# Loading the overflow experts of a mixture-of-experts stage from SyncE at a register address

## The reference

```python
g_w, g_idx = lax.top_k(pg, 1)                 # one of 4 groups
e_w, e_idx = lax.top_k(pe, EXP_TOPK)          # two of its 8 experts
for g in range(N_GROUPS):
    h = silu(xf @ w_eg[g]) * (xf @ w_eu[g])   # per expert: 1024 x 128, twice
    out = out + (h * gate) @ w_ed[g]          # per expert: 128 x 1024
```

## Time and profile before

| | |
|---|---|
| median of 3 runs | 1450.25 us (1449.45 to 1452.43) |
| profiled execution, own time | 1453.34 us |
| its span | 1451.5 us |
| PE busy | 1316.5 us, 91% of the span |
| DVE, ACT, POOL busy | 37%, 23%, 15% |
| DMA, mean over the span | 142 GB/s, 205.63 MB |
| mixture steps, layer 0 | about 573 to 709 us |
| mixture steps, layer 1 | about 1280 to 1421 us |

### The profile page before, as it was taken

The page is one execution under the profiler, slowest core; times in us unless marked ns, Lnnn a source line. Parts: engine busy times, 40 slices in busy tenths (PEclk is TensorE's granted clock), DMA queues, the critical chain, the costliest instruction groups (busy, mean ns, idle before and its releaser), DMA issues.

```text
span 1451.5 us, 15494 instructions
## 1 busy us (share of the span) xinstructions
PE 1316.5 (91%) x5756; PEld 729.4 (50%) x5756; DVE 534.1 (37%) x1542; ACT 339.4 (23%) x773; POOL 222.4 (15%) x304
## 2 busy tenths in 40 slices
PE   7999998999999998988699999999999999989780
PEld 5654446544444555655484544564444445556550
DVE  1278885110111137221335779731101113552115
ACT  2142467100000100222213326641000010012121
POOL 5011033000000001223241100600000000023313
PEclk9999999999999997999899999999999999979995
DMA  8302102503303305999662120061060061289966
GB/s 239 116 13 59 58 1 71 174 1 89 128 0 135 154 31 178 396 407 376 233 166 64 45 63 17 20 182 44 0 217 0 0 261 44 85 304 411 406 237 240
DMA packets 95485, 205.63 MB, mean 142 GB/s; under 512 B 26465, under 2 KB 35905, under 8 KB 95409
## 3 DMA queue, kind: packets, MB, share of 16 engines
q1 hardware_dynamic: 80800, 178.13, 34.7%
q0 software_dynamic: 14608, 26.49, 5.2%
HBM read 196.29 MB, written 27.78 MB: 154 GB/s over the span
## 4 chain that ended last, share of the span: by engine, by line
PE 79%; DVE 5%; DMA 4%; ACT 4%; issue 4%; PEld 1%; POOL 1%; PEldq 1%; SPq 0%; POOLq 0%; ACTq 0%; DVEq 0%
PE bank L748 34%; PE bank L1030 10%; PE bank L1081 10%; PE bank L1127 7%; PE bank L1138 4%; PE bank L1114 2%; PE bank L781 2%; DMA uv<-xd,mb 2%; DVE mb L1462 2%; PE bank L830 1%; PE bank L1047 1%; PE bank L734 1%; PE bank L834 1%; PE bank L1122 1%; PE bank L934 1%
## 5 line engine op out<-in xcount | busy, mean ns | idle before, releaser
L748 PE MATMUL bank<-ring,xt 128*128 128x512 f32 (+1 forms) x1120 | 434.0, 544 | 7.9 <-DMA ring<-in_w_in 5.1
L748 PEld LDWEIGHTS bank<-ring,xt 128*128 128x128 f32 x1120 | 214.3, 194 | 209.5 <-issue 190.0
L1751 DVE TENSOR_TENSOR scr<-scr,bank 128x512 f32<-128x512 f32 x20 | 13.7, 687 | 368.6 <-PE bank L1030 368.6
L1081 PE MATMUL bank<-ring,xt 128*128 128x512 f32 x320 | 141.3, 595 | 0.0
L542 POOL TENSOR_SCALAR stat<-stat 128x1 f32<-128x1 f32 (+1 forms) x27 | 11.7, 434 | 796.2 <-ACT uv L1214 614.0
L1358 ACT ACTIVATE scr<-bank,stat 128x512 f32<-128x512 f32 x40 | 25.3, 683 | 347.9 <-PE bank L748 347.9
L1081 PEld LDWEIGHTS bank<-ring,xt 128*128 128x128 f32 x320 | 59.4, 191 | 66.9 <-issue 66.9
L1030 PE MATMUL bank<-ring,att 128*128 128x512 f32 x160 | 72.5, 596 | 2.2 <-ACT sgt L1350 1.8
L781 PE MATMUL bank<-ring,xt 128*128 128x512 f32 x160 | 73.7, 593 | 0.0
L1030 PE MATMUL bank<-ring,sgt 128*128 128x512 f32 x160 | 71.9, 592 | 0.0
L748 PE MATMUL bank<-more,xt 128*128 128x512 f32 x160 | 70.3, 592 | 0.0
(11 more groups left out here) (284 smaller groups left out, 1819.9 us busy)
## 6 DMA issues: line engine op xcount, KB each, us to landing
ring<-in_w_in SPq DMA_DIRECT2D x12, 2048.0 KB, 9.3
ring<-in_w_ed SPq DMA_DIRECT2D x32, 512.0 KB, 17.7
ring<-in_w_eg SPq DMA_DIRECT2D x26, 512.0 KB, 10.5
ring<-in_w_eu SPq DMA_DIRECT2D x26, 512.0 KB, 17.2
ring<-in_w_out SPq DMA_DIRECT2D x4, 2048.0 KB, 12.6
more<-in_w_ed SPq DMA_DIRECT2D x14, 512.0 KB, 10.9
qkv<-in_w_eg SPq DMA_DIRECT2D x12, 512.0 KB, 7.4
qkv<-in_w_eu SPq DMA_DIRECT2D x12, 512.0 KB, 10.1
```

The source lines that it names most:

```text
L748: mm = pe.matmul(out, xt[:, k, t * P:(t + 1) * P], rhs[:, k, :], start=(k == 0), stop=(k == KD - 1))
L1081: mm = pe.matmul(banks[5 + n % 3][:, :], xt[:, k, t * P:(t + 1) * P], w[:, k, :], start=(k == 0), stop=(k == KD - 1))
```

## The change

The loads of units 28 and 29 move from POOL to SP. They stand in SP's order of units, between unit 27 and unit 30, and are plain DMAs whose row is a register: SP waits for `experts_known` before the first refill and loads two expert numbers from `over_expert` into registers. POOL's six indirect DMAs go away, and with them DVE's five operations for `over_rows`; the signal `over_rows_ready` stays and now stands behind the second part of the row table, and POOL waits for it before gather 14. TensorE waits for `up_in` and `down_in` in step 14 as in all others. The load now takes place whether or not there is an overflow unit: `over_expert` is the number of experts that start at or before the unit, less one, which is 31 where there is none.

```diff
-LOADED = [e for e in range(2 * NB) if e // 2 != OVER_AT]
+LOADED = list(range(2 * NB))
...
                 expert(9, EXPERTS * L + 9)
+                sp.wait_ge(experts_known, prior("experts_known", L) + 1)
+                over_row = [sp.value_load(over_expert[:, h:h + 1], min_val=0, max_val=EXPERTS - 1) for h in range(ALWAYS)]
+
+                def row_of(v):
+                    if v // 2 == OVER_AT:
+                        return EXPERTS * L + over_row[v % 2]
+                    return EXPERTS * L + 2 * BLOCK_AT[v // 2] + v % 2
+
                 for e in range(PLACES, 2 * NB, 2):
-                    units = [v for v in (e, e + 1) if v in LOADED]
+                    units = [v for v in (e, e + 1) if v < 2 * NB]
                     for v in units:
                         sp.wait_ge(gu_psum[L], (v - PLACES) // 2 + 1)
-                        expert_up(v % PLACES, EXPERTS * L + 2 * BLOCK_AT[v // 2] + v % 2, up_in[v % PLACES])
+                        expert_up(v % PLACES, row_of(v), up_in[v % PLACES])
                     for v in units:
                         sp.wait_ge(y_psum[L], (v - PLACES) // 2 + 1)
-                        expert_down(v % PLACES, EXPERTS * L + 2 * BLOCK_AT[v // 2] + v % 2, down_in[v % PLACES])
-                sp.wait_ge(experts_known, prior("experts_known", L) + 1)
+                        expert_down(v % PLACES, row_of(v), down_in[v % PLACES])
...
                 for b in range(NB):
+                    if b + XBUF == OVER_AT:
+                        pool.wait_ge(over_rows_ready, L + 1)
                     if b + XBUF < NB:
                         pool.wait_ge(h_done[L], b + 1)
                         gather(b + XBUF, b % XBUF, x_in[b % XBUF])
                     pool.wait_ge(y_ready[L], b + 1)
                     scatter(b, b % XBUF, b % YBUF, y_out[b % YBUF])
-                    if b == OVER_AT - PLACES // 2:
-                        pool.wait_ge(over_rows_ready, L + 1)
-                        for v in range(ALWAYS):
-                            i = (2 * OVER_AT + v) % PLACES
-                            for dst, w, landed_sem in ((places[i][0][:, 0:1024], "w_eg", more_up),
-                                                       (places[i][0][:, 1024:2048], "w_eu", more_up),
-                                                       (places[i][1], "w_ed", more_down)):
-                                rows = (a[w].rearrange("l g e f d -> (l g e f) d") if w == "w_ed" else
-                                        a[w].rearrange("l g e (p k) f -> (l g e p) (k f)", k=KD))
-                                pool.indirect_dma_start(out=dst, out_offset=None, in_=rows,
-                                                        in_offset=bass.IndirectOffsetOnAxis(ap=over_rows[:, v:v + 1], axis=0),
-                                                        bounds_check=DEPTH * EXPERTS * P - 1, oob_is_err=False
-                                                        ).then_inc(landed_sem, 16)
...
-                        if b != OVER_AT:
-                            pe.wait_ge(up_in[e % PLACES], 32 * filled(e % PLACES, L, e))
-                        else:
-                            pe.wait_ge(more_up, 32 * ALWAYS * (L + 1))
+                        pe.wait_ge(up_in[e % PLACES], 32 * filled(e % PLACES, L, e))
...
-                few = [P, ALWAYS, EXPERTS]
-                then(V.tensor_tensor(over_hot, over(start[:, 0:EXPERTS], ALWAYS, 1, few),
-                                     ids[:, 0:ALWAYS].unsqueeze(2).broadcast_to(few), ALU.is_le))
-                V.tensor_scalar(over_none, ids[:, 0:ALWAYS], start[:, EXPERTS:EXPERTS + 1], NOWHERE, ALU.is_ge, ALU.mult)
-                then(V.tensor_reduce(over_begun, over_hot, AX.X, ALU.add))
-                then(V.scalar_tensor_tensor(over_begun, over_begun, float(P), over_none, ALU.mult, ALU.add))
-                V.tensor_scalar(over_rows, over_begun, ids[:, BR:BR + 1], float(P * (EXPERTS * L - 1) - 1),
-                                ALU.add, ALU.add).then_inc(over_rows_ready, 1)
+                V.nop().then_inc(over_rows_ready, 1)
```

More of the change, by code:

```diff
@@ L259, in build @@
         n_over = ALWAYS + 2 * REST
[L260 to L263, removed]
         over_expert = mbv(AT_OVER, n_over)[0:1, :].bitcast(I32)
@@ L324, in build @@
         x_over, y_over = sem("x_over"), sem("y_over")
-        more_up, more_down, over_rows_ready = sem("more_up"), sem("more_down"), sem("over_rows_ready")
+        over_rows_ready = sem("over_rows_ready")
         params, ln_loaded, wr_loaded = sem("params"), sem("ln_loaded"), sem("wr_loaded")
@@ L1175, in down_step @@
                         e = 2 * b + h
[L1176 to L1179, removed]
+                        pe.wait_ge(down_in[e % PLACES], 16 * down_loads(e % PLACES) * filled(e % PLACES, L, e))
                     down(two_of(b), b % 2)
```

## The result

| | before | after |
|---|---|---|
| median | 1451.34 us (1448.56 to 1456.65, 6 runs) | 1461.65 us (1460.73 to 1464.79, 6 runs) |
| ratio to before | 1 | 1.0071 (95% interval 1.0054 to 1.0087) |
| profiled execution, span | 1451.5 us | 1463.0 us |

A forecast was written before the change was run, and what follows sets the result against it. Weight traffic through full DMA engines was taken as the bound in the mixture steps. Layer 0: 7.8 - 0.65 - 0.9 + 1.5 = 7.7 us; layer 1: 3.9 - 0.3 = 3.6; together 11.3, from 1450.25 to 1461.5 us, range 1454 to 1467.

The forecast's parts named there:

- The bytes: Overflow loads per layer go from 0 and 1 to 2 and 2, adding 3.15 MB and 1.57 MB; chance 0.84 that this decides.
- The price of the bytes: Added loads ahead of units 30 to 33, at 403 GB/s, delay later weights 7.8 us in layer 0, 3.9 in layer 1.
- The empty packets: Dropping POOL's out-of-bounds gather packets frees DMA time: 0.65 us gained in layer 0, 0.3 in layer 1.
- The slack of 0.9 us: In layer 0 unit 33's last weights land 0.9 us before the last up projection, absorbing that much delay.
- POOL at nothing: Removing POOL's six indirect DMAs ahead of gather 14 gains nothing, since weights bind behind it; up to 3.8 us otherwise.
- SP and DVE at nothing: SP's wait, register loads and extra issues, and DVE's five dropped operations, were costed at nothing.
- TensorE's clock: Layer 0's last step runs at the slow clock after a wait, costing 1.5 us; layer 1 already pays it.
- The sum: Both layers' mixture steps: 7.7 us later in layer 0 and 3.6 in layer 1, together 11.3 us.
- No change: Rival: the added loads are hidden by room in the drain at the steps' end, time 1450 us; chance 0.07.
- POOL as the bound: Rival: POOL's weight gathers hold up gather 14, so removing them saves 3.8 us, time 1446.5 us; chance 0.05.
- SP can't keep up: Rival: register-address loads hold SP so its DMA queue runs dry, some 5 us more, 1466 to 1470 us; chance 0.04.

The follow-up runs named there:

- e3: Kernel before, with POOL's indices always in bounds so POOL loads two overflow experts per layer; 1464.13 us, ratio 1.0091.
- e5: Changed kernel with a constant row (expert 31 of the layer) instead of the register for units 28 and 29; 1462.76 us, ratio 1.0071.
- e1: Changed kernel with the loads of units 28 and 29 left out; 1447.18 us, ratio 0.9971.
- e2: Kernel before, with POOL's six indices always beyond the bound, so no overflow weights move; 1448.41 us, ratio 0.9987.
- e7: Changed kernel with the two dropped semaphores more_up and more_down declared again, unused; 1462.19 us, ratio 1.0068.
- e8: Changed kernel with DVE's five operations per layer for over_rows put back, result unread; 1462.78 us, ratio 1.0073.
- e6: Changed kernel with each load of units 28 and 29 under a branch on SP, issued only if that overflow unit exists; 1451.27 us, ratio 1.0000.
- e10: Kernel before with POOL's six weight gathers one step later, behind gather 14; 1457.52 us, ratio 1.0029.
- e9: Changed kernel with DVE's five operations and six indirect DMAs per layer on POOL put back, moving nothing; 1466.08 us, ratio 1.0098.
- e4: Changed kernel without the loads of unit 29, so one overflow expert per layer; 1452.95 us, ratio 1.0016.

## Why the prediction was right, point by point

**The bytes.** Right. Layer 0's POOL queue moves 9.09 MB before and after, so it held no overflow weights. e3 shows that the loss comes with the bytes from either queue (from POOL's by another path, through gather 14), e5 that it doesn't come with the register, e1 that it goes with the bytes.

**The price of the bytes.** Forecast 7.8 - 0.65 us later landing in layer 0 and 3.9 - 0.3 in layer 1; in the profiles it is 8.6 and 4.2, or 4.2 to 4.3 us per added expert where I took 3.9. The Trainium skill's figure (DMA: Bandwidth & Descriptors, Specifications), with which I had estimated 8.8 and 4.4, came nearer to these two landings, although the engines move 405 GB/s from 656 to 690 us in the changed kernel too. It isn't a general rate: the same bytes by POOL (e2 to e3) come 7.1 and 6.1 us later for two, 3.3 us per expert, and by the ratios 15 us for four experts, 3.8 each. By SP (e1 to after) the landings of the two layers move by 17.3 us together for four experts, 4.3 each, while the ratios give only 14.5 us, 3.6 each; PE's lateness in e1 hides 3.7 us. So at the landing an expert costs 4.2 to 4.3 us in SP's queue and 3.3 in POOL's, around the 3.9 of 403 GB/s, and why the two differ was not found out. That the time of the kernel is near 3.9 per expert isn't a confirmation of the rate.

**The empty packets.** I had credited 0.65 and 0.3 us for them. 864 packets without data went away in layer 0 (5184 to 4320). From before to after no gain can be seen: the landings are later than 3.9 us per expert would make them. The one pair with equal bytes points the forecast way: without the empty packets (e1) unit 33 lands 0.2 and 1.2 us earlier than with them (e2). But kernels of equal work differ by as much (120.3 to 121.9 in after, e5, e7 and e8). Not shown.

**The slack of 0.9 us.** Right: the last up projection starts at the landing in both layers.

**POOL at nothing.** Right in the mixture: e6, which frees POOL at the bytes of before, gains nothing there, nor does e1 against e2 (1.7 us slower), and in layer 0 of e10 the wait moves from the gather to the weights. It holds only while POOL's gathers carry few weights; with two experts in them, in e3, gather 14 is on the chain. And the step overlooked that fewer DMAs on POOL shorten the end of the program, by 2.9 us (e9 against e8). That is one of the two largest errors of the sum (the other is the clock, below), and both favour the change.

**SP and DVE at nothing.** Right (e5, e8).

**TensorE's clock.** This step failed in its size and place. I gave layer 0 the 1.5 us that the slow clock cost in layer 1 before. In the changed kernel the last step has a granted clock of 1.00, the 2.4 GHz level, in layer 0, and in both layers takes 6.85 us from up to down, so layer 0 lost nothing and layer 1 gained 1.45 us. The waits ahead of it are 1.34 and 1.53 us, where it was 2.79 in layer 1 before. In the other runs it took 6.85 us after waits of 0.3 to 2.7 us, and in e8, after 2.9 and 3.2 us, 8.4 and 9.8 us, with a granted clock of 0.50, the 1.2 GHz level, for the first 2.4 and 5.5 us (below, layer 1). So in these traces the penalty comes and goes with how long PE waits there, which I could not have taken from one row.

```profile
1416.50:1422.00 5.50, 5.50 (x39) 5.50 (x41) 0.00 (x0) 0.00 (x0) 0.00 (x0) 0.50 0.08 26
```

**The sum.** Layer 0: forecast 7.7, profile 7.8. This agreement is luck: the weights came 1.5 us later than forecast, and the 1.5 us of the clock didn't come. Layer 1: forecast 3.6, profile 2.7 (4.15 for the later start, 1.45 back from the clock). The end of the program: forecast nothing, profile -3.0. This gives 7.5 us, and the measured 10.3 us have an interval of 7.8 to 12.6. In the three profiled executions of kernels with the work of the changed one (after, e5, e7) the mixture takes 255.8 to 256.9 us, which makes it 7.5 to 8.6. In e8, whose added operations are hidden, it takes 259.2 because of the clock, so this penalty is there in some executions and not in others; how often, these single profiles can't say. So the forecast of 11.3 was near the measured value partly because I didn't know of a gain of 2.9 us, while about 2 us of the measured loss are not placed by the three profiles, and of before there is only one.

**The rivals.** No change: against it e1, e3, e4. But it had a grain of truth: where weights aren't late PE is, so from e1 to e4 the landing moves by 5.6 us per layer and the last up projection only by 3.8. POOL as the bound: against it e6, and e10 in layer 0. SP can't keep up: against it e3 and e5.

## What to carry to other kernels

Count what an indirect load really moves before replacing it: with indices beyond the bound it is also a condition, and a plain load at a register address moves its bytes every time. In a stretch where all DMA engines are full, a load costs about its bytes at the stretch's rate (here 3.3 to 4.3 us per expert where 403 GB/s gives 3.9), whoever issues it and however cheap the issue is. A wait that ends just ahead of another wait is worth nothing: find out which one ends last before removing the first.

## What was not expected of the hardware

- The end of the program, after the last DMA issue and with no instruction in the trace, takes 6.3 us when POOL issues twelve further indirect DMAs in the kernel, and 3.5 us when not, even if these move nothing (e9 and e8). It is in the span and in the measured time.
- A gather in POOL's queue behind six weight loads took 14.9 us from issue to landing (e3) where the same gather takes 7.2 us in the changed kernel. In e10 one took 12.3 us.
- Step 13's up projection takes 3.67 us at full clock (layer 1 before, granted clock 1.00). After a single wait of 2.95 to 3.56 us it took 6.2 to 6.6 us in nine cases, 5.0 to 5.2 in three and 3.67 in one (layer 1 of e5). Where the wait was cut in two by eight transposes, 2.3 to 2.5 us together (both layers before and of e2, layer 1 of e9), it took 5.0 to 5.4 us in four cases and 3.67 in one, and after a single wait of 2.47 us (layer 0 of e10) 5.04. After single waits of 0.8 to 1.7 us (layer 0 of e5, e7 and e9) it was 3.67. So longer waits mostly come with a slower step behind them, but not always, and these runs don't tell whether joining two waits into one costs anything beyond their length.
